# Recurrence of two heads: block-diagonal 128x128 products against pairs of 64x64 products

## What is computed

```
def rwkv7_scan(r, w, k, v, kk, a):
    decay = jnp.exp(-jnp.exp(w))
    b = kk * a
    def step(S, inp):
        r_t, d_t, k_t, v_t, kk_t, b_t = inp
        sa = jnp.einsum('bhij,bhj->bhi', S, -kk_t)
        S = S * d_t[:, :, None, :] + sa[..., None] * b_t[:, :, None, :] + v_t[..., None] * k_t[:, :, None, :]
        return S, jnp.einsum('bhij,bhj->bhi', S, r_t)
...
for d in range(N_DIR):            # forwards, and on the flipped sequence
    y_sum = y_sum + rwkv7_scan(...)
```

## Time and profile before

| what | us |
|---|---|
| median of 3 runs | 3860.27 (3858.74 to 3861.18) |
| span of the profiled execution | 3861.1 |
| of that, the six pairs of the recurrence (399.15 to 880.00) | 480.85 |
| PE busy | 3690.7 (96%) |
| DVE busy | 2330.1 (60%) |
| ACT busy | 1636.5 (42%) |
| POOL busy | 522.0 (14%) |

### The profile page before, as it was taken

One profiled execution on the slowest core, in us unless ns is written; L12 is line 12 of the kernel. 1 busy time (PEld: TensorE's weight loads), 2 busy tenths in 40 slices (PEclk: granted clock), 3 DMA queues, 4 the chain that ended last, 5 costly groups with the idle time before them and its releaser, 6 DMA issues.

```text
span 3861.1 us, 79816 instructions
## 1 busy us (share of the span) xinstructions
PE 3690.7 (96%) x30206; PEld 3651.0 (95%) x30206; DVE 2330.1 (60%) x3113; ACT 1636.5 (42%) x2173; POOL 522.0 (14%) x532
## 2 busy tenths in 40 slices
PE   6999999999999999989999999999999699999996
PEld 6998999999999999989999999999999699999996
DVE  6787666566566547776654545566666554545454
ACT  4456232224444443564443434443344343434343
POOL 5000344430002000130100000010000600000006
PEclk9999999999999999999999999999999899999998
DMA  5444212113565555445555555555544355555553
GB/s 204 159 158 143 62 48 65 43 54 126 179 201 182 187 183 175 153 141 164 184 186 175 189 179 185 177 183 185 184 155 153 120 169 181 188 180 186 175 188 127
DMA packets 165374, 605.65 MB, mean 157 GB/s; under 512 B 18384, under 2 KB 18512, under 8 KB 164992
## 3 DMA queue, kind: packets, MB, share of 16 engines
q1 hardware_dynamic: 163296, 594.62, 47.8%
q10 hardware_dynamic: 1760, 7.00, 0.5%
q0 software_dynamic: 192, 2.23, 0.2%
HBM read 601.67 MB, written 2.10 MB: 156 GB/s over the span
## 4 chain that ended last, share of the span: by engine, by line
PE 83%; DVE 9%; POOL 3%; ACT 2%; issue 2%; ACTq 0%; POOLq 0%; DVEq 0%
PE bank L311 25%; PE bank L312 25%; PE bank L313 25%; PE bank L1214 5%; DVE w_lo L300 3%; POOL ln_acc L2545 1%; POOL ln_d L2543 1%; POOL ln_acc L2548 1%; POOL ln_sq L2546 1%; ACT w_hi L291 0%; DVE xa L1793 0%; ACT X L2585 0%; DVE hx L370 0%; DVE mem_hl L370 0%; DVE abd L1126 0%
## 5 line engine op out<-in xcount | busy, mean ns | idle before, releaser
L291 ACT ACTIVATE w_hi<-raw 128x1024 fp32r<-128x1024 f32 x1130 | 1160.6, 1052 | 976.6 <-PE bank L313 957.2
L300 DVE TENSOR_TENSOR w_lo<-raw,w_hi 128x1024 fp32r<-128x1024 f32 x1130 | 1374.1, 1255 | 101.4 <-ACT w_hi L291 101.2
L311 PE MATMUL bank<-u,w_hi 128*128 128x256 f32 (+1 forms) x2304 | 656.7, 285 | 9.5 <-DVE w_lo L300 9.5
L312 PE MATMUL bank<-u,w_hi 128*128 128x256 f32 (+1 forms) x2304 | 657.1, 285 | 0.0
L313 PE MATMUL bank<-u,w_lo 128*128 128x256 f32 (+1 forms) x2304 | 656.9, 285 | 0.0
L311 PE MATMUL bank<-hid,w_hi 128*128 128x256 f32 x2048 | 579.8, 283 | 0.0
L312 PE MATMUL bank<-hid,w_hi 128*128 128x256 f32 x2048 | 579.6, 283 | 0.0
L313 PE MATMUL bank<-hid,w_lo 128*128 128x256 f32 x2048 | 579.6, 283 | 0.0
L311 PE MATMUL bank<-xh,w_hi 128*128 128x256 f32 x1808 | 515.0, 285 | 19.4 <-issue 15.3
L312 PE MATMUL bank<-xh,w_hi 128*128 128x256 f32 x1808 | 512.8, 284 | 0.0
L313 PE MATMUL bank<-xh,w_lo 128*128 128x256 f32 x1808 | 512.8, 284 | 0.0
(11 more groups left out here) (457 smaller groups left out, 6080.9 us busy)
## 6 DMA issues: line engine op xcount, KB each, us to landing
raw<-stream SPq DMA_DIRECT2D x1130, 512.0 KB, 4.0
x_raw<-xT ACTq DMA_DIRECT2D x4, 512.0 KB, 10.3
mem_raw<-memT ACTq DMA_DIRECT2D x4, 512.0 KB, 18.4
x_res<-xT POOLq DMA_DIRECT2D x1, 2048.0 KB, 8.9
out<-X SPq DMA_DIRECT2D x4, 512.0 KB, 2.6
cst<-consts ACTq DMA_DIRECT2D x1, 1696.0 KB, 15.4
w_sb<-w ACTq DMA_DIRECT2D x1, 384.0 KB, 20.0
a_sb<-a ACTq DMA_DIRECT2D x1, 384.0 KB, 20.4
```

What stands on the lines that cost most here:

```text
L291: nc.scalar.activation(w_hi[:, slot], raw[:, slot], ACT.Copy).then_inc(hi_ready, 1)
L300: nc.vector.tensor_tensor(w_lo[:, slot], raw[:, slot], w_hi[:, slot].bitcast(F), ALU.subtract).then_inc(lo_ready, 1)
L311: nc.tensor.matmul(dst, w_hi[:, slot, j], hi, start=first, stop=False)
L312: nc.tensor.matmul(dst, w_hi[:, slot, j], lo, start=False, stop=False)
```

## The change

Instead of one product of block-diagonal 128x128 squares, each chunk gets two products of 64x64, one for each head: head 0 on partitions 0 to 63 into PSUM partitions 0 to 63, head 1 on partitions 64 to 127 into PSUM partitions 64 to 127 of the same bank. Each uses a quarter of the array, the two on the diagonal. The operands lose their zeros and are half as wide: `[P, NCH, CH]` in place of `[P, NCH, P]`. So one instruction of DVE or POOL writes both heads, results are 128x256 instead of 128x512, nothing need be zeroed, and the buffers that shared memory now have their own. The transposes become products with an identity (`istack`). `m` is masked at once with the mask of level 0, which takes one POOL instruction out of each direction. The dense blocks are spread otherwise: 7 instead of 4 in each Gram part, none in the levels, and one is left over for the end of the pair. The units of the third tile are split in levels 2 and 3 and not before the last level. PE's loop over the pairs is written out six times.

```
-GO_START, GO_PREP, GO_GRAM, GO_LEVEL, GO_STEP = 8, 24, 4, 1, 1
+GO_START, GO_PREP, GO_GRAM, GO_STEP = 8, 24, 7, 1
...
-            for k, n in enumerate(("abd", "rbd", "bbd", "kbd", "mt", "tm", "brt", "btok", "ktok")):
-                w[n] = at(f"{n}{d}", o + 2 * K * k, [P, NCH, P])
-            w["nkatv"] = at(f"nkatv{d}", o + 18 * K, [P, NCH, CH])
-            w["u"], w["x"], w["kat"], w["krt"] = w["kbd"], w["bbd"], w["btok"], w["ktok"]
-            w["ml"] = v_bd if d == 0 else at("ml1", o + 19 * K, [P, NCH, P])
+            for k, n in enumerate(("abd", "rbd", "bbd", "kbd", "mt", "tm", "brt", "btok", "ktok", "nkatv", "kat", "krt", "u", "x", "ml")):
+                w[n] = at(f"{n}{d}", o + K * k, [P, NCH, CH])
...
-                    for h in halves():
-                        last = nc.gpsimd.tensor_tensor(w["kbd"][h, :, h], chunks(w["kd"][h]), chunks(w["e3"][h]), ALU.mult)
-                    rw_o.done(last, f"kbd{d}")
+                    rw_o.done(nc.gpsimd.tensor_tensor(w["kbd"][:], chunks(w["kd"][:]), chunks(w["e3"][:]), ALU.mult), f"kbd{d}")
...
-                    rw_o.done(nc.gpsimd.tensor_tensor(w["tm"][:], w["tm"][:], level(0), ALU.mult), f"t0_{d}")
-                    need(pool, rw_o, f"t0_{d}", p)
...
 (ACT)
                 for l in LV:
-                    if l == LEVELS - 1:
-                        split_hi(act, pair_tile(p, 2).later())
                     for d, w in enumerate(dirs):
...
-                        rw_a.done(nc.scalar.activation(w["x"][:], blocks(bank_of(d, 1)), ACT.Copy), f"X{l}_{d}")
+                        rw_a.done(nc.scalar.activation(w["x"][:], value_part(bank_of(d, 1), 0), ACT.Copy), f"X{l}_{d}")
+                    if l in TILE_2:
+                        split_hi(act, pair_tile(p, 2).later(), (TILE_2.index(l),))
...
 (DVE)
-                    for h in halves():
-                        last = nc.vector.tensor_tensor(w["bbd"][h, :, h], chunks(w["bb"][h]), chunks(w["e3"][h]), ALU.mult)
-                    rw_v.done(last, f"bbd{d}")
+                    rw_v.done(nc.vector.tensor_tensor(w["bbd"][:], chunks(w["bb"][:]), chunks(w["e3"][:]), ALU.mult), f"bbd{d}")
...
 (PE)
-            with pe.Fori(0, PAIRS) as p:
+            for p in range(PAIRS):
                 go = pe_pair_tiles(pe, p)
-                def each(bank, lhs, rhs, n=P, o=0):
+                def heads2(out, lhs, rhs, start=True, stop=True):
+                    for h in halves():
+                        last = nc.tensor.matmul(out[h], lhs[h], rhs[h], start=start, stop=stop)
+                    return last
+                def each(bank, lhs, rhs, o=0):
                     for c in range(NCH):
-                        last = nc.tensor.matmul(bank[:, o + n * c:o + n * c + n], lhs[:, c], rhs[:, c], start=True, stop=True)
+                        last = heads2(bank[:, o + CH * c:o + CH * c + CH], lhs[:, c], rhs[:, c])
                     return last
                 def turned(bank, src):
                     for c in range(NCH):
-                        last = nc.tensor.transpose(bank[:, P * c:P * c + P], src[:, c], const("ident"))
+                        last = heads2(bank[:, CH * c:CH * c + CH], src[:, c], const("istack"))
                     return last
...
                         rw_p.done(each(bank_of(d, 1), w["ml"], w["tm"]), f"X{l}_{d}")
-                    go(GO_LEVEL)
```

More of the change, by code:

```diff
@@ L146, in constants @@
                       for b in range(NB)], 1)
-    up = same & (s[:, None] < s[None, :])
     incl = same & (s[:, None] <= s[None, :])
-    levels = [same & (s[:, None] >> (l + 1) == s[None, :] >> (l + 1))
-              & (s[:, None] >> l != s[None, :] >> l) for l in range(LEVELS)]
+    c = np.arange(CH)[None, :]
+    up, lo = s[:, None] < c, s[:, None] > c
+    levels = [(s[:, None] >> (l + 1) == c >> (l + 1)) & (s[:, None] >> l != c >> l) for l in range(LEVELS)]
     t = np.arange(T)
@@ L918, in dve_kk @@
                     kk_v.done(last, f"kk{b}")
[L920 to L927, removed]
-                for m in (dirs[d]["abd"], dirs[d]["rbd"], dirs[d]["bbd"], dirs[d]["kbd"]):
-                    nc.gpsimd.memset(m[:], 0.0).then_inc(zeroed, 1)
         LV = range(1, LEVELS)
@@ L993, in four @@
         def four(ap):
-            return ap.unsqueeze(1).broadcast_to([P, NCH, P])
-        def blocks(bank):
-            return bank[:].rearrange("p (c t) -> p c t", c=NCH)
+            return ap.unsqueeze(1).broadcast_to([P, NCH, CH])
         def value_part(bank, k):
@@ L1003, in level @@
         def level(l):
-            return four(const("levels")[:, P * l:P * l + P])
+            return four(const("levels")[:, CH * l:CH * l + CH])
         def halves():
@@ L1012, in pool_rwkv @@
         def pool_rwkv(pool):
-            pool.wait_ge(zeroed, 9)
+            need(pool, at_p, f"pv{A_T + X_T - 1}")
+            pool.wait_ge(agate_out, A_T + X_T)
             pool.wait_ge(in_lora, 48)
@@ L1055, in pool_rwkv @@
                 need(pool, rw_p, f"X{LEVELS - 1}_1", p)
+        TILE_2 = (2, 3)
         def act_rwkv(act):
@@ L1124, in dve_rwkv @@
                     need(v, rw_a, f"e3{d}", p)
-                    for h in halves():
-                        last = nc.vector.tensor_tensor(w["abd"][h, :, h], kkn[h, p].rearrange("p (c t) -> p c t", c=NCH),
-                                                       chunks(w["e2"][h]), ALU.mult)
-                    rw_v.done(last, f"abd{d}")
-                    for h in halves():
-                        last = nc.vector.tensor_tensor(w["bbd"][h, :, h], chunks(w["bb"][h]), chunks(w["e3"][h]), ALU.mult)
-                    rw_v.done(last, f"bbd{d}")
+                    rw_v.done(nc.vector.tensor_tensor(w["abd"][:], chunks(kkn[:, p]), chunks(w["e2"][:]), ALU.mult), f"abd{d}")
+                    rw_v.done(nc.vector.tensor_tensor(w["bbd"][:], chunks(w["bb"][:]), chunks(w["e3"][:]), ALU.mult), f"bbd{d}")
                     end = CH - 1 if d == 0 else 0
@@ L1233, in pe_rwkv @@
                 need(pe, rw_o, "vbd", p)
-                for c in range(NCH):
-                    last = nc.tensor.matmul(bank_of(0, 2)[:, CH * c:CH * c + CH], v_bd[:, c], const("istack"), start=True, stop=True)
-                rw_p.done(last, "vtok0")
+                rw_p.done(turned(bank_of(0, 2), v_pair), "vtok0")
                 go(GO_PREP)
@@ L1291, in pe_rwkv @@
                             need(pe, rw_v, f"S{s - 1}_{d}", p)
-                            rw_p.done(nc.tensor.matmul(bank_of(d, 0)[:, 0:CH], w["abd"][:, chunk_of(d, s)], st[d][:, old],
-                                                       start=True, stop=True), f"W{s}_{d}")
+                            rw_p.done(heads2(bank_of(d, 0)[:, 0:CH], w["abd"][:, chunk_of(d, s)], st[d][:, old]), f"W{s}_{d}")
                     if s > 0:
@@ L1303, in pe_rwkv @@
                         rhs = w["nkatv"][:, c] if s == 0 else ws[d][:]
-                        rw_p.done(nc.tensor.matmul(bank_of(d, 1)[:, 0:CH], w["u"][:, c], rhs, start=True, stop=True), f"SA{s}_{d}")
+                        rw_p.done(heads2(bank_of(d, 1)[:, 0:CH], w["u"][:, c], rhs), f"SA{s}_{d}")
                     go(GO_STEP)
```

86 lines of the change are left out of this document (41 added, 45 removed).

## The result

The changed kernel takes 3747.62 us (median; 3744.87 to 3749.24) against 3860.05 (3858.74 to 3861.18): a ratio of 0.9709, 95% interval 0.9695 to 0.9723. The forecast was 3746.

The account below looks back on a forecast made before the run. PE, busy for 96% of the span, was taken to bound all but the preparation (DVE and POOL). Parts of 11.5, 17.6, 15.4 and 16.5 make 61.0 us a pair against 80.03, giving 3746 us, range 3724 to 3795.

Parts of the forecast that it names:

- A product: One full-width product on PE, 0.89 us before, would cost 8 x 0.058 = 0.46 us with both quarters running at once.
- The first rival: The two quarters don't run at once: a product costs 0.93 us, a pair 85.5, total 3890; chance 0.10.
- Changing over: Switching PE between whole-array dense blocks and quarter products costs 0.2 us each way, 0.40 there and back.
- Preparation: First part of a pair, bound by DVE and POOL: from 14.21 to 11.5 us, PE's remaining wait 1.2.
- Gram: Second part of a pair: from 20.13 to 17.6 us, the pieces giving 17.1 plus 0.5 for a wait.
- stay about covered by the 7 blocks: In Gram, DVE's masks and POOL's eight instructions would be about hidden behind 7 dense blocks; 0.5 us added for a wait.
- Levels: Third part of a pair: from 28.75 to 15.4 us, being 12.9 of products, 1.2 of waits and 1.3 for the last level.
- the likeliest thing to make this part longer: DVE's splitting of two units in levels 2 and 3, 1.2 us each or more, fills DVE in a 3 us level.
- Steps and crossing: Last part of a pair: from 16.94 to 16.5 us; chunk products fall to 0.116, but 20 changes cost 4.0.
- Clock: Granted clock 1.00 in all pair windows; a rival of 0.50 through the levels gave 3815, chance 0.04.
- Fetching: Instruction fetch for the written-out loop: nothing taken, at most 10 us kept for the range.
- The sum: The four parts make 61.0 us a pair against 80.03; six pairs take 367.9 instead of 480.85, 113 us gained.

Follow-up runs that it names:

- e1: Changed kernel with both heads' products made in head 0's quarter, one behind the other, same instruction count; 3904.68 us, ratio 1.0112.
- e11: The changed kernel with every product in the upper left quarter, twice as many one behind the other, run again for its trace; 3886.33 us in one execution.
- e3: Changed kernel, but each product issues all 4 chunks of head 0 before the 4 of head 1; 3777.00 us, ratio 0.9782.
- e7: Changed kernel with DVE splitting the tile's first unit ahead of the bonus instructions and the second behind the first Gram masks; 3742.31 us, ratio 0.9697.
- e6: Changed kernel with no dense blocks within the steps and 10 instead of 7 in each Gram part; 3749.12 us, ratio 0.9716.
- e4: Kernel before, with only PE's loop over the six pairs written out; 3857.77 us, ratio 0.9993.
- e2: Kernel before with only PE changed: full-width products become two 64x64 quarter products, loop written out, other engines still 512 wide; 3831.50 us, ratio 0.992.
- e5: Changed kernel with dense blocks spread as before (4 per Gram part, single ones in levels), third tile split before the last level; 3754.18 us, ratio 0.9722.
- e10: Changed kernel with each product in two groups, two chunks of head 0 then two of head 1, and again; 3749.62 us, ratio 0.9714.
- e9: Changed kernel with the blocks behind the second and third Gram parts spread over the six products ahead, ten more places a pair; 3764.82 us, ratio 0.9751.

## Why the prediction was right

**A product**: 0.46 forecast, 0.467 measured. The reasoning (half of the load, half of the stream, and two quarters at once because the earlier trace rows shows it for rows and for columns) holds, and e1 and e11 show that the second quarter gives the factor of two. What the prediction took from the earlier trace rows too widely is the remark that the order of the halves doesn't matter: e3 puts 16 instructions ahead and loses a quarter of the pace. The changed kernel writes the heads in turn, so the sum was not touched.

The first rival had for it that no row shows two row halves writing one PSUM bank. The run after shows two quarters that do, those on the diagonal: both write one bank, and take 0.467 a product against 0.93 one behind the other (e11).

**Changing over**: 0.40 there and back forecast, 0.33 measured, in and out unequal (0.20 and 0.14, estimates). The 283.17 from which the forecast counts agrees with the next dense matmul of the trace before, which starts at 283.28, 0.11 later. With some 14 places a pair it is a term of nearly 5 us, and worth having been counted.

**Preparation**: 11.5 forecast, 11.39 measured. `abd` and `bbd` of direction 0 take 1.4 and not 1.8. Of the wait 0.8 is left and not 1.2.

**Gram**: 17.6 forecast, 17.90 measured. Without waits it is 16.95 (e7), where the pieces gave 17.1. The 0.5 for a wait was put on DVE's masks and POOL; the wait is 0.95 and stands elsewhere, at a dense block whose unit DVE hasn't split. The step that failed is "stay about covered by the 7 blocks": it asked what the products wait for, not what the blocks themselves wait for, now that the six products ahead are 2.5 us shorter.

**Levels**: 15.4 forecast, 15.07 measured: 28 x 0.467 = 13.1, and 2.0 of waiting: some 0.35 in each of the four levels from the second on (0.3 forecast), 0.3 in the first, and 0.33 at the end, where 1.3 was forecast. Of the chain's terms, the 0.2 called pipeline and the 0.1 were the author's estimates, with no row named for them. In the trace after, ACT starts 0.29 behind the end of X's 0.467 (616.43 to 616.72), DVE 0.23 behind the end of T's (618.16 to 618.39), and X's load 0.12 behind the end of `tm` (616.59 to 616.71). The 1.3 was too large: a further wait (0.41, before the second SA) falls into the steps, and even with it the end is 0.74. The units split in levels 2 and 3, "the likeliest thing to make this part longer", cost 0.03 each.

**Steps and crossing**: 16.5 forecast, 16.62 measured. The prediction has the trips between quarters and blocks at 4.0 and says that they are paid although they cover latencies. They are paid and not saved by taking them out (e6). But ten trips at 0.33 are 3.3, so the term was 0.7 too large, and waits that the pieces didn't have (PE idles for 1.03 us of this part) made up for it. That the part came out to 0.1 is luck.

**Clock**: forecast 1.00 in all pairs, and so it is. The reason given, that no wait reaches the 3.4 us ahead of the slow stretch before, isn't shown: e4 keeps the long wait, and most of its pairs have no slow stretch, while e2 has new ones. The stretch costs 1.6 in Gram (e4), but a pair loses only 1.2 to 1.4 by it, and the prediction's pattern, the fourth pair, is one of the four of six that have it. **Fetching**: nothing taken, nothing found (e4). **The first pair**: 62.1 forecast (61.0 + 1.9 - 0.8), 62.63 measured.

**The sum**: 113.8 forecast for the pairs (480.85 less 62.1 and five times 61.0), 112.1 measured. It was right by its parts: the largest miss of a part is 0.33 us in 15.4. That the misses cancel, 0.30 too little in Gram and 0.33 too much in the levels, to 61.0 against 60.98 is luck; added up without sign they would be 5 us in all. The 1.7 between forecast and measured come from the first pair (0.5 above its forecast) and the last (62.9, which the sum counted as 61.0), less 0.75 because the stretch before ends at 880.75 here and at 880.00 in the earlier trace rows. One thing the sum hides is where the gain sits. It can be read as a gain of PE, and e2 says that PE alone gets 28 of 112 us. Most of the rest came with the halved instructions of POOL, DVE and ACT (e2 to e5), which the prediction counted where it made the chain of a level (0.42 for 0.69 and 0.60) but gave no price of its own.

## What to carry to other kernels

When two halves or quarters of the array are to work at once, write their instructions in turn, or at most four matmuls of one ahead of the other (e10: 0.467 us a product; e3, with eight ahead: 0.575), and put full-array work in few large groups: each trip cost 0.33 us in e9, and nothing in the steps, where PE would wait anyway (e6). When PE's part becomes twice as fast, look through every engine that feeds it for work of the old width, and look at the filler work too: it has inputs of its own that used to be covered. A sum by parts is worth making even where one number would do, since each part can then be found wrong alone.

## What the runs showed of the hardware

Not expected: that matmuls of two quarters start out of the program's order (e3, `krt` at 622.66 ahead of `kat` at 622.71), and the limit on how far a second quarter's instruction may stand behind. With 4 or 8 instructions of the first head ahead a product costs 0.467 us, with 16 ahead 0.575, with both in one quarter 0.93. Beside POOL, DVE's `bbd` of 256 numbers took 0.96 us, and alone 0.41 (593.35 and 595.17 of after); which speaks for a gain on DVE by POOL's fewer instructions, though no run here separates it. And by the rows at 603.95 to 607.74 of after, going into the whole array from quarters takes longer (0.20) than coming out (0.14); e9 gives 0.33 for both.
